# Expert rows of u and v by one gather, expert work in groups of four rows, output projections normed tile by tile

## What is computed

```python
q = (hb @ wq).reshape(tc, PEER_HEADS, 2, PEER_HALF)
s = jnp.einsum('thpk,hpnk->thpn', q, keys)
s_top, i_top = lax.top_k(s, PEER_TOPK)
...
eid = jnp.take_along_axis(cid.reshape(tc, PEER_HEADS, -1), pos, -1)
g = jax.nn.softmax(best.astype(jnp.float32), -1).astype(hb.dtype)
act = jax.nn.gelu(jnp.einsum('td,thed->the', hb, u[eid]), approximate=False)
return jnp.einsum('the,thed->td', g * act, v[eid])
```

## Time and profile before

| | us |
|---|---|
| median of 3 runs | 3879.05 |
| lowest and highest | 3877.84, 3880.47 |
| the profiled execution, its time | 3882.43 |
| its span | 3880.6 |
| busy: PE, VectorE (DVE), ScalarE (ACT), GpSimd (POOL) | 3090.4, 1930.3, 736.8, 1439.3 |
| mean granted clock of TensorE, share of full speed | 0.89 |

### The profile page before, as it was taken

How to read it: one execution, slowest core, us unless ns; L and a number is a source line. 1 busy time by engine, 2 the same in 40 slices (tenths; PEclk the granted TensorE clock), 3 DMA queues, 4 the chain that set the end, 5 groups by cost and what they waited for, 6 DMA issues and landing times. The chain is left out here.

```text
span 3880.6 us, 27858 instructions
## 1 busy us (share of the span) xinstructions
PE 3090.4 (80%) x8564; PEld 1527.7 (39%) x8564; DVE 1930.3 (50%) x4721; ACT 736.8 (19%) x1716; POOL 1439.3 (37%) x1540
## 2 busy tenths in 40 slices
PE   8987766878878888787668665888887597897888
PEld 3444433333333333333233334334332354553663
DVE  1136547666666676776330648666765224223000
ACT  0112312222122121221100412222221120122000
POOL 0000006777777777777400004777777000000000
PEclk9996878999999989999879787999999798998999
DMA  5143209999999999999812237999999442333333
GB/s 189 55 152 109 90 33 362 419 420 420 415 416 414 418 414 411 419 406 419 318 63 89 86 134 282 419 419 420 415 416 418 163 141 103 110 109 130 108 130 119
DMA packets 348743, 1026.06 MB, mean 264 GB/s; under 512 B 53686, under 2 KB 58294, under 8 KB 346534
## 3 DMA queue, kind: packets, MB, share of 16 engines
q0 software_dynamic: 221184, 805.40, 51.2%
q1 hardware_dynamic: 126984, 217.63, 15.9%
q10 hardware_dynamic: 432, 1.31, 0.1%
HBM read 1023.10 MB, written 1.13 MB: 264 GB/s over the span
## 5 line engine op out<-in xcount | busy, mean ns | idle before, releaser
L1423 PE MATMUL l_peer_experts_acc<-l_peer_experts_ring,l_peer_experts_diag 128*128 128x512 f32 x3072 | 1490.5, 636 | 358.6 <-ACT l_peer_experts_diag L1463 292.3
L1598 DVE SCALAR_TENSOR_TENSOR weight_slots<-weight_slots,l_peer_experts_h 128x1024 f32<-128x1024 f32 x768 | 937.1, 1220 | 590.9 <-DMA weight_slots<-in_peer_u,l_peer_experts_picks 584.3
L1356 POOL DMA_INDIRECT weight_slots<-in_peer_u,l_peer_experts_picks x768 | 719.7, 937 | 1291.2 <-DVE l_peer_experts_picks L1550 1041.0
L1423 PEld LDWEIGHTS l_peer_experts_acc<-l_peer_experts_ring,l_peer_experts_diag 128*128 128x128 f32 x3072 | 606.1, 204 | 1193.5 <-issue 1003.6
L1361 POOL DMA_INDIRECT l_peer_experts_ring<-in_peer_v,l_peer_experts_picks x768 | 719.4, 937 | 299.1 <-issue 201.4
L1463 ACT ACTIVATE l_peer_experts_diag<-const_ident,l_peer_experts_wgt 128x128 f32<-128x128 f32 x768 | 229.5, 387 | 172.5 <-DVE l_peer_experts_wgt L1566 172.5
L1386 PE MATMUL l_peer_experts_queries<-h_t,l_query_weights 128*128 128x512 f32 (+3 forms) x576 | 180.5, 457 | 3.6 <-PEq L61 3.6
L1445 ACT ACTIVATE l_peer_experts_h<-h_tiles 128x1024 f32<-128x1024 f32 x48 | 49.3, 1027 | 612.6 <-DVE weight_slots L1598 612.6
L1386 PEld LDWEIGHTS l_peer_experts_queries<-h_t,l_query_weights 128*128 128x128 f32 x576 | 104.7, 197 | 75.7 <-issue 67.0
L1442 ACT ACTIVATE l_peer_experts_soft<-l_peer_experts_best,l_peer_experts_low 128x16 f32<-128x16 f32 x48 | 14.7, 307 | 578.6 <-DVE l_peer_experts_low L1529 578.6
L192 PE MATMUL b_mlp_acc<-weight_slots,b_up 128*128 128x512 f32 x256 | 113.1, 605 | 12.1 <-DVEq L287 12.1
(11 more groups left out here) (434 smaller groups left out, 3220.9 us busy)
## 6 DMA issues: line engine op xcount, KB each, us to landing
weight_slots<-in_w_mod SPq DMA_DIRECT2D x24, 2048.0 KB, 7.7
weight_slots<-in_w_in SPq DMA_DIRECT2D x20, 2048.0 KB, 7.5
l_query_weights<-query_weights SPq DMA_DIRECT2D x16, 1024.0 KB, 7.7
weight_slots<-in_w_mlp_up SPq DMA_DIRECT2D x8, 2048.0 KB, 7.6
weight_slots<-in_w_mlp_down SPq DMA_DIRECT2D x8, 2048.0 KB, 7.6
weight_slots<-in_peer_u,l_peer_experts_picks POOLq DMA_INDIRECT x768, 8.9
l_peer_experts_ring<-in_peer_v,l_peer_experts_picks POOLq DMA_INDIRECT x768, 8.9
weight_slots<-in_gla_w_in SPq DMA_DIRECT2D x6, 2048.0 KB, 7.9
```

The lines of the kernel that those rows point to most:

```text
L1356: pool.indirect_dma_start(u_ring[:, k % RING, :], None, u, bass.IndirectOffsetOnAxis(ap=picks[:, b % 4, k:k + 1], axis=0)).then_inc(landed ...
L1423: ins = nc.tensor.matmul(acc[:, c * BANK:(c + 1) * BANK], diag[:, k, :], v_ring[:, k % RING, c * BANK:(c + 1) * BANK], start=(k == 0), sto ...
L1598: nc.vector.scalar_tensor_tensor(row, row, 1.0, hp[:, :], ALU.mult, ALU.mult, accum_out=dots[:, b % 2, k:k + 1]).then_inc(dotted, 1)
```

## The change

- **Experts.** u and v are laid side by side on the host (`expert_rows`, rows of 8 KB), so one gather brings both rows of an expert: 768 gathers of 1 MB instead of 1536 of 512 KB. A ring of 10 slots holds them (4 in `weight_slots`, 6 in `ring`), each held until TensorE has added the group of four rows to which its row belongs. Dots become Gelus, weights, diagonals and sums in groups of four rows within the same step: v is no longer one step behind u. `diag` has 8 matrices instead of 16. The last step's sum is taken at k = 3. ACT copies the next step's tokens between Gelu and diagonals of the last group, the exponentials stand behind group 2's diagonals.
- **Projections.** `stage_out_norm` projects a tile, and norms it while the next is projected; the keys are turned after the second tile. It loads rows, keys and the first query weights at its start. One barrier less.
- **mod0.** Four matmuls at four column groups of the array instead of one for each k, and the four partial sums added by the matrix that turns them; the bias is cleared on all 128 partitions first, and SP's loads wait for that.
- **b_sq** is gone: the squares are made tile by tile in b_mlp1.

```diff
+                if square:
+                    def squares(t, n0, width, half, turn):
+                        dst = flat[:, where(n0, 0, width // P * n_tok)]
+                        dve.wait_ge(act_out, t + 3)
+                        nc.vector.tensor_tensor(dst, dst, dst, ALU.mult)
...
+                sp.wait_ge(bias_cleared, 1)
+                sp.dma_start(bias_sb[0:2, :, :].rearrange("c i n -> c (i n)"), bias[0:n_tiles * BANK].partition_broadcast(2)).then_inc(bias_loaded, 16)
...
-                    for k in range(KC):
-                        last = nc.tensor.matmul(ps[0:2, i % 2, :], silu_c[:, k, 0:2], weights.slots[:, slot, k, :], start=(k == 0), stop=(k == KC - 1))
+                    for n in range(2):
+                        for j in range(4):
+                            last = nc.tensor.matmul(ps[32 * j:32 * j + 32, i % 2, :], silu_c[:, 2 * j + n, :], weights.slots[:, slot, 2 * j + n, :],
...
+                nc.vector.memset(bias_sb[:, :, :], 0.0).then_inc(bias_cleared, 1)
...
+def stage_out_norm(nc, name, weights, act_t, x, y, tiles, rows, ident, h, h_t, keys, loads=()):
...
+                project(0)
+                project(1)
+                turn(None)
+                for i in range(2, n):
+                    project(i)
+                    turn(i - 2)
...
+                for i, (m, ym) in enumerate(tiles):
+                    dve.wait_ge(multiplied, i + 1)
...
+UV_SLOTS = 10
...
-        v_ring = st.sb("ring", [P, RING, D])
-        u_ring = slots.rearrange("p s k n -> p (s k n)").rearrange("p (s d) -> p s d", d=D)
+        shared = slots.rearrange("p s k n -> p (s k n)").rearrange("p (s d) -> p s d", d=2 * D)
+        more = st.sb("ring", [P, UV_SLOTS - 4, 2 * D])
...
-        diag = st.sb("diag", [P, TOPK, P])
+        diag = st.sb("diag", [P, DIAGS, P])
...
+        def rows(step, k, half):
+            slot = (before0 + step * TOPK + k) % UV_SLOTS
+            both = shared[:, slot, :] if slot < 4 else more[:, slot - 4, :]
+            return both if half is None else both[:, half * D:(half + 1) * D]
...
             @block.gpsimd
             def _(pool):
-                for b in range(steps + 1):
-                    if b < steps:
-                        pool.wait_ge(chosen, b + 1)
+                for b in range(steps):
+                    pool.wait_ge(chosen, b + 1)
                     for k in range(TOPK):
-                        if b < steps:
-                            if b * TOPK + k >= RING:
-                                pool.wait_ge(dotted, b * TOPK + k - RING + 1)
-                            pool.indirect_dma_start(u_ring[:, k % RING, :], None, u, bass.IndirectOffsetOnAxis(ap=picks[:, b % 4, k:k + 1], axis=0)).then_inc(landed[k % RING], 16)
-                        if b:
-                            if (b - 1) * TOPK + k >= RING:
-                                pool.wait_ge(added, ((b - 1) * TOPK + k - RING) // 2 + 1)
-                            pool.indirect_dma_start(v_ring[:, k % RING, :], None, v, bass.IndirectOffsetOnAxis(ap=picks[:, (b - 1) % 4, k:k + 1], axis=0)).then_inc(landed[RING + k % RING], 16)
+                        n = b * TOPK + k
+                        if n >= UV_SLOTS:
+                            pool.wait_ge(added, (n - UV_SLOTS) // 4 + 1)
...
-                for b in range(steps + 1):
-                    if not b:
-                        score(3)
-                        continue
-                    step = b - 1
-                    if step:
-                        pe.wait_ge(sum_taken, step)
+                for b in range(steps):
+                    if b:
+                        pe.wait_ge(sum_taken, b)
                     for k in range(TOPK):
-                        if k == RING and b + 3 < steps:
+                        if k == TOPK // 2 and b + 3 < steps:
                             score(b + 3)
-                        if k in (3, RING + 1):
+                        if k in (3, TOPK // 2 + 1):
                             next(later, None)
-                        pe.wait_ge(landed[RING + k % RING], landing(step, k))
                         if k % 4 == 0:
-                            pe.wait_ge(diag_ready, step * TOPK // 4 + k // 4 + 1)
+                            pe.wait_ge(diag_ready, b * TOPK // 4 + k // 4 + 1)
+                        row = rows(b, k, 1)
                         for c in range(2):
-                            ins = nc.tensor.matmul(acc[:, c * BANK:(c + 1) * BANK], diag[:, k, :], v_ring[:, k % RING, c * BANK:(c + 1) * BANK],
+                            ins = nc.tensor.matmul(acc[:, c * BANK:(c + 1) * BANK], diag[:, k % DIAGS, :], row[:, c * BANK:(c + 1) * BANK],
                                                    start=(k == 0), stop=(k == TOPK - 1))
-                        if k % 2:
+                        if k % 4 == 3:
                             ins.then_inc(added, 1)
...
-                for b in range(steps + 1):
-                    if b:
-                        step = b - 1
-                        act.wait_ge(w_ready, step + 1)
-                        for k in range(TOPK):
-                            if k % 4 == 0 and step:
-                                act.wait_ge(added, (step - 1) * TOPK // 2 + k // 2 + 2)
-                            scaled = nc.scalar.activation(diag[:, k, :], ident, ACT.Copy, scale=wgt[:, step % 2, k:k + 1])
-                            if k % 4 == 3:
-                                scaled.then_inc(diag_ready, 1)
-                    if b + 2 < steps:
-                        exps(b + 2)
-                    if b:
-                        done = [before + (b + i) * 2 // group for i in (-1, 0)]
-                        take(min(done[0], len(units)), min(done[1], len(units)))
-                    if b < steps:
-                        act.wait_ge(dotted, (b + 1) * TOPK)
-                        if b + 1 < steps:
+                for b in range(steps):
+                    for j in range(TOPK // 4):
+                        four = b * TOPK // 4 + j
+                        cols = slice(4 * j, 4 * j + 4)
+                        act.wait_ge(dotted, 4 * four + 4)
+                        nc.scalar.activation(gel[:, b % 2, cols], dots[:, b % 2, cols], ACT.Gelu).then_inc(gelu_done, 1)
+                        if j == TOPK // 4 - 1 and b + 1 < steps:
                             tile_in(b + 1)
-                        nc.scalar.activation(gel[:, b % 2, :], dots[:, b % 2, :], ACT.Gelu).then_inc(gelu_done, 1)
+                        if four >= DIAGS // 4:
+                            act.wait_ge(added, four - DIAGS // 4 + 1)
+                        act.wait_ge(w_ready, four + 1)
+                        for k in range(4 * j, 4 * j + 4):
+                            scaled = nc.scalar.activation(diag[:, k % DIAGS, :], ident, ACT.Copy, scale=wgt[:, b % 2, k:k + 1])
+                        scaled.then_inc(diag_ready, 1)
+                        if j == 1 and b:
+                            done = [before + (b + i) * 2 // group for i in (-1, 0)]
+                            take(min(done[0], len(units)), min(done[1], len(units)))
+                        if j == 2 and b + 2 < steps:
+                            exps(b + 2)
...
-                def weigh(step):
-                    dve.wait_ge(gelu_done, step + 1)
+                def weigh(step, j):
+                    cols = slice(4 * j, 4 * j + 4)
+                    dve.wait_ge(gelu_done, step * TOPK // 4 + j + 1)
                     dve.wait_ge(chain, links)
-                    nc.vector.tensor_tensor(wgt[:, step % 2, :], gel[:, step % 2, :], share[:, step % 2, :], ALU.mult).then_inc(w_ready, 1)
+                    nc.vector.tensor_tensor(wgt[:, step % 2, cols], gel[:, step % 2, cols], share[:, step % 2, cols], ALU.mult).then_inc(w_ready, 1)
...
-                    dve.wait_ge(added, (step + 1) * TOPK // 2)
+                    dve.wait_ge(added, (step + 1) * TOPK // 4)
...
-                for b in range(steps + 1):
-                    if b == steps:
-                        if b > 1:
-                            take(b - 2)
-                        weigh(b - 1)
-                        take(b - 1)
-                        continue
+                for b in range(steps):
                     dve.wait_ge(h_ready, b + 1)
                     for k in range(TOPK):
-                        dve.wait_ge(landed[k % RING], landing(b, k))
-                        row = u_ring[:, k % RING, :]
+                        dve.wait_ge(*landing(b, k))
+                        row = rows(b, k, 0)
                         nc.vector.scalar_tensor_tensor(row, row, 1.0, hp[:, :], ALU.mult, ALU.mult, accum_out=dots[:, b % 2, k:k + 1]).then_inc(dotted, 1)
-                        if k == 1:
-                            if b > 1:
-                                take(b - 2)
-                            if b:
-                                weigh(b - 1)
+                        if k == 3 and b:
+                            take(b - 1)
```

(10 more changed lines are left out.)

192 lines of the change are left out of this document (129 added, 63 removed).

## The result

The changed kernel takes 4129.4 us (median of 4 runs, 4117.8 to 4136.0), the kernel before 3879.8 beside it: ratio 1.064, interval 1.062 to 1.067. It is slower, by 250 us, and 69 us above the upper end of the forecast range. The profiled execution took 4132.0 us, its span is 4130.2.

The account below looks back on a forecast made before the run. Expert stages were taken as DMA-bound, 40.8 us a step. The new slot loop at 44.05 us a step adds 131 us, the short places give back 53: +78, 3957 us by the median; own range 3920 to 3994, full range 3790 to 4060.

Parts of the forecast that it names:

- the loop through the slots: Expert stages: group g+2 waits for slots of group g, twice a step; 41.2 us, 44.05 with one clock loss.
- the short places: Outside the expert loop: projection and norm in ab_out 26.4 and c_out 11.3, squares 8, mod0 7 us gained; together -53.
- the wait before group 2: TensorE's wait in the slot loop, put at 4.2 us; its possible 1.8 us clock loss was left out of the forecast.
- freed to landed: Slot loop, from slot release to second row landed: 4.1 lone gather, 1.25 more bytes, 2.4 second row; 7.75 us.
- I count the first each step and the second as a case: Clock loss before group 0, 2.85 us, counted every step; that before group 2, 1.8 us, left to a rival.
- both waits pay: Rival: clock lost before groups 0 and 2 in each step, S = 45.85, 4040 us; chance 0.17.
- Group 0's hop: Slot loop on TensorE: 16 matmuls 6.9, query projection piece 1.7, clock loss 2.85 us.
- the two hops from dot to PE: Slot loop, dot to TensorE's matmuls: 3.35 us to group 2, 4.70 to group 0 with taken sum and weights.
- S: Length of one expert step in us, forecast 44.05; both expert stages together last 118.2 + 46 S.
- the signs that the prediction named: Expert trace: gathers in fours released by TensorE, 4 to 6 us waits before group 0, DMA share near 0.93, 44 us steps.
- The rival of faster gathers: Expert stages: loop latencies hide and a 1 MB row takes 2.45 us, S = 39.2, 3734 us; chance 0.10.

Follow-up runs that it names:

- the short places alone: Changed kernel with the expert stages and two tables of the kernel before put back: 3819.4 us beside 3881.7, ratio 0.984; 4087.8 beside 4155.1 on the other kind of chip.
- two gathers for a row: Changed kernel with slots freed by pairs, each row brought by two 512 KB gathers: 4111.4 us (kernel before 4154), 3863.2 on the other kind (3882).
- with pairs: Changed kernel with slots freed after every second row instead of every fourth: 3839.5 us first run (kernel before 4155.1), 3829.5 second (3879.9, ratio 0.987).
- single rows: Changed kernel with slots freed row by row and the last sum taken at k = 2: 3815.9 us, ratio 0.983 to the kernel before.

## Why the prediction was wrong

The direction and the place held: the loop through the slots is the step, and the short places give about what was said. The time did not: +250 us instead of +78, 4129 against a range that ended at 4060. Two terms of the loop failed, the wait before group 2, whose clock was put at nothing, and "freed to landed", which was too small. By its hops, in the step shown and as the mean over the steps of layer 0:

| hop of the loop, us | predicted | step shown | mean |
|---|---|---|---|
| group 0 on PE, with the clock lost | 11.45 | 10.87 | 10.6 |
| released to second row there | 7.75 | 8.90 | 8.9 |
| dot to group 2 on PE | 3.35 | 3.08 | 3.1 |
| group 2 on PE | 9.05 | 11.39 | 11.0 |
| released to second row there | 7.75 | 9.04 | 9.2 |
| dot, taken sum, weights to group 0 on PE | 4.70 | 4.82 | 4.8 |
| step | 44.05 | 48.10 | 47.6 |

- **The step that failed first is a choice, not a price**: "I count the first each step and the second as a case". The wait before group 2 was drawn as 4.2 us and is 4.95 (5.0 in the mean, never under 4.2 in layer 0); it cost 2.3 us in the step shown and 1.9 in the mean, near the 1.8 of the rival, and in every step. The reason given, that stretched groups leave the gathers time, was argued from nothing in the trace. The rival "both waits pay", 4040 us, had this part right, and was still 89 us too low by the next term.
- **The term that was too small**: "freed to landed", 7.75, measured 8.90 and 9.04. It was built of one gather that landed alone in an empty machine (4.1) plus bytes. The first row of a burst (the four gathers that one group sets free) did come near to that (5.4 and 5.9 after its release, 5.35 predicted), the second 3.2 to 3.5 us later instead of 2.4. The four gathers of a burst are issued 1.24 us apart, twice as fast as DMA moves them, so the second shares the engines with its followers; that this is the cause was not tried by itself. The page of the kernel before held a warning that was not used, 8.9 us from issue to landing as the median of all gathers of u (part 6), against the 4.1 in the earlier trace rows from which the term was built. Two hops of 1.2 us are 2.4 us a step, 2.6 in the mean.

```profile
weight_slots<-in_peer_u,l_peer_experts_picks POOLq DMA_INDIRECT x768, 8.9
```

- Together these two are 4.8 us (2.34 + 2.44). Group 0's hop is 0.6 shorter than was said, since its clock cost 1.9 us and not 2.85, behind a longer wait, and the two hops from dot to PE are 0.15 shorter, which leaves 4.05 in the step shown and 3.6 in the mean of layer 0. Over both stages S is 47.8 for 44.05: 46 x 3.8 = 174 us, and the short places took 2 of it back; the forecast missed by 172. This is the account of a step and not a promise of what each term is worth: with both clock losses gone, 4.1 us, the kernel gained only 2.7 a step.
- Of the signs that the prediction named, the gathers in fours and the waits are there, but PE waits 7 us before group 0 and not 4 to 6, and DMA share is 0.87 and not 0.93.
- **The short places**, -53: 62 less in the experiment, 55 in the trace of the changed kernel. ab_out gave 32 and not 26, half of it because the turns of the keys and of the first tile keep PE 1.8 and 0.9 us from its next projection (last two rows of the first fence) where 3.7 and 2.0 were said; mod0 gave 6.8, and that 7 was said is in part luck, for it was the middle of 0 to 12 with no row behind it; c_out's stage 11 from its projection to the queries (11.3 said), squares 8.8 (8). These are 59. The trace has 55 because from the end of the first expert stage to c_out's projection 379.9 us pass, 374.9 in the kernel before and 374.6 in the run of the short places alone; where these 5 us go was not traced. The rows are those of PE's first matmul behind each place, of c_out's projection, and one of the kernel before for mod0:

```profile
47.53 12.81 PE L191 MATMUL ab_v_acc<-weight_slots,h_t 128*128 128x512 f32 x24 [6.35 <-DVEq L280]
...
530.01 5.42 PE L1496 MATMUL l_peer_experts_queries<-h_t,l_query_weights 128*128 128x128 f32 x32 [1.96 <-PEq L61]
...
2467.55 27.70 PE L786 MATMUL c_out_acc<-weight_slots,h_t 128*128 128x512 f32 x64 [1.84 <-PEq L61]
...
2509.83 5.38 PE L1496 MATMUL l_peer_experts_queries<-h_t,l_query_weights 128*128 128x128 f32 x32 [1.96 <-PEq L61]
...
4005.24 5.12 PE L191 MATMUL b_mlp_acc<-weight_slots,b_up 128*128 128x512 f32 x8 [3.88 <-DVEq L280]
...
485.18 1.91 PE L801 MATMUL ab_out_turned<-const_ident,l_keys 128*128 128x128 f32 x16
...
500.66 1.04 PE L801 MATMUL ab_out_turned<-const_ident,h_tiles 128*128 128x128 f32 x8
```

```profile
54.32 2.05 PE L192 MATMUL ab_v_acc<-weight_slots,h_t 128*128 128x512 f32 x2 [6.08 <-DVEq L287]
```

- **The rival of faster gathers** (3734) was right that larger gathers move more (427 GB/s) and wrong that they can with 10 slots freed by fours (352 GB/s). The Trainium skill, "DMA: Bandwidth & Descriptors", section Rules for kernel authors, asks for transfers of 1 MiB and more for the highest bandwidth. The runs agree by a little: 427 GB/s with gathers of 1 MB whose slots are free after the dot, 415 with gathers of 512 KB in the kernel before, though a row's length changed with it.
- The Trainium skill, "TensorE: Matmul & The Clock Gate", section HAM oscillation, tells of a kernel whose every tile restarts cold behind its DMA wait. The trace of the changed kernel agrees, twice a step: granted clock 0.52 behind 7.28 us of waiting and 0.50 behind 4.95.

## What to carry to other kernels

When a buffer is held until the last engine is done with it, write down the loop freed - issued - landed - computed - freed, count how many rows of the next group wait for this group, and take the landing time from a loaded stage, not from a transfer that ran alone. Free slots in a smaller unit than the group that is computed: here pairs instead of fours turned 6% slower into 1.3% faster. And if PE's wait stands in the loop, the clock that it costs stands there too; matmuls of zeros in that wait gave 45 us even where DMA's share was already 0.99.

## What the runs showed of the hardware

- The kernel before takes 3876 to 3888 us on some of the chips and 4142 to 4168 on others, the changed kernel 4116 to 4136 on one of each. What differs is the expert stage with gathers of 512 KB, of 4-KB rows: the expert stage of the kernel before moved 415 GB/s at share 1.02 and, on a chip of the other kind, 365 at 0.95 (first fence, the short places alone); with two gathers for a row it was 406 on the one kind and 368 on the other (second and third fence), where gathers of 1 MB, of 8-KB rows, moved 427 on that same kind of chip. Why was not found.

```profile
1000.00:1400.00 400.00, 299.54 (x646) 127.50 (x645) 239.49 (x619) 81.38 (x199) 255.80 (x273) 0.87 0.95 365
```

```profile
1000.00:1400.00 400.00, 329.80 (x728) 142.41 (x726) 275.40 (x712) 96.51 (x245) 286.50 (x306) 0.93 1.01 406
```

```profile
1000.00:1400.00 400.00, 309.42 (x667) 133.26 (x665) 246.72 (x640) 86.85 (x221) 259.68 (x277) 0.89 0.97 368
```

- Matmuls of zeros ahead of PE's waits held the granted clock of the expert window at 0.97 to 1.00, where it was 0.85 in the changed kernel, 0.94 with pairs and 0.91 with single rows.
- The length of a wait did not tell by itself whether the clock was lost: behind 2.79 us it was 0.50 in the kernel before, behind 3.06 us (at 1270.54 in the first run with pairs) it stayed at 1.00.
